# Two edits to a two-layer hybrid backbone kernel: query and gate units of the last layer's projection without context columns, and the recurrent stage's level products on VectorE

## The reference

```python
IN_SIZES = (HG_W, HG_W, HG_W, HG_W, HG_W, GQA_W, GQA_KV_W, GQA_KV_W, NA_W, NA_W, NA_W)
# = 256 x5 (q, f_fwd, f_bwd, i, g) | 384, 128, 128 (q, k, v) | 384 x3 (q, k, v)
for l in range(DEPTH):
    need_ctx = l < DEPTH - 1
    ...
    y_lat, y_ctx = mixing_sublayer(...)      # y_ctx is None if not need_ctx
```

## Time and profile before

| | |
|---|---|
| median of 3 runs | 4626.42 us (4623.34 to 4635.23) |
| the profiled execution, its own time | 4631.18 us |
| its span, first to last instruction | 4629.5 us |
| mean granted TensorE clock | 0.905 of full |
| PE busy, DVE, ACT, POOL | 83%, 44%, 23%, 11% of the span |
| `project_in(1)` | from 2560 to 2903 us in the span, 343 us |
| `hgrn` of layer 0 | from 457 to 639 us, 182 us |
| `hgrn` of layer 1 | from 2909 to 3058 us, 149 us |

### The profile page before, as it was taken

One profiled execution on the slowest core, in us unless ns is written; L12 is line 12 of the kernel. 1 busy time (PEld: TensorE's weight loads), 2 busy tenths in 40 slices (PEclk: granted clock), 3 DMA queues, 4 the chain that ended last, 5 costly groups with the idle time before them and its releaser, 6 DMA issues. The chain is left out here.

```text
span 4629.5 us, 55289 instructions
## 1 busy us (share of the span) xinstructions
PE 3859.6 (83%) x22802; PEld 3059.9 (66%) x22802; DVE 2037.8 (44%) x2175; ACT 1087.3 (23%) x1434; POOL 492.6 (11%) x314
## 2 busy tenths in 40 slices
PE   3998468939785999999996899469767859999996
PEld 2887336438674888888884788345356647777774
DVE  3111657645423343444345121667656234544445
ACT  1000332425314111111114000332345131111113
POOL 1000403002005000000003000511022040000000
PEclk6999679968897999999997999679889879999998
DMA  5222430041223101111105222240132211111111
GB/s 185 82 82 79 156 134 21 12 108 23 86 77 123 42 27 41 41 35 32 41 18 164 80 82 78 104 141 5 46 82 68 66 63 51 41 54 41 51 35 73
DMA packets 339917, 320.39 MB, mean 69 GB/s; under 512 B 42718, under 2 KB 310602, under 8 KB 339786
## 3 DMA queue, kind: packets, MB, share of 16 engines
q1 hardware_dynamic: 297514, 265.07, 18.5%
q0 software_dynamic: 6912, 31.46, 2.3%
q10 hardware_dynamic: 35360, 22.02, 1.5%
HBM read 248.17 MB, written 73.30 MB: 69 GB/s over the span
## 5 line engine op out<-in xcount | busy, mean ns | idle before, releaser
L477 PE MATMUL psum<-h_hi,f_whi 128*128 128x512 f32 (+1 forms) x1760 | 485.1, 373 | 70.7 <-DVE f_wlo L922 70.7
L927 DVE TENSOR_TENSOR y<-y,psum 128x1280 f32<-128x1280 f32 (+1 forms) x352 | 476.8, 1355 | 109.3 <-PE psum L477 103.9
L477 PE MATMUL psum<-h_lo,f_whi 128*128 128x512 f32 (+1 forms) x1760 | 481.6, 371 | 0.0
L477 PE MATMUL psum<-h_hi,f_wlo 128*128 128x512 f32 (+1 forms) x1760 | 481.4, 371 | 0.0
L477 PE MATMUL psum<-h_hi,w_hi 128*128 128x512 f32 x1472 | 379.2, 364 | 118.2 <-DVE w_lo L543 118.2
L477 PEld LDWEIGHTS psum<-h_hi,f_whi 128*128 128x128 f32 x1760 | 306.8, 188 | 135.0 <-DVE f_wlo L922 71.2
L477 PE MATMUL psum<-h_lo,w_hi 128*128 128x512 f32 x1472 | 377.4, 363 | 0.0
L477 PE MATMUL psum<-h_hi,w_lo 128*128 128x512 f32 x1472 | 377.0, 362 | 0.0
L922 DVE TENSOR_TENSOR f_wlo<-f_raw,f_whi 128x1024 fp32r<-128x1024 f32 x132 | 161.0, 1221 | 481.9 <-ACT f_whi L893 423.5
L477 PEld LDWEIGHTS psum<-h_hi,w_hi 128*128 128x128 f32 x1472 | 249.9, 190 | 164.3 <-issue 119.1
L893 ACT CAST f_whi<-f_raw 128x1024 fp32r<-128x1024 f32 x132 | 138.4, 1048 | 907.3 <-PE psum L477 882.5
(11 more groups left out here) (264 smaller groups left out, 5706.9 us busy)
## 6 DMA issues: line engine op xcount, KB each, us to landing
f_raw<-in_w_ffn_in SPq DMA_DIRECT2D x88, 512.0 KB, 6.0
proj_cm<-lin_stage POOLq DMA_DIRECT2D x48, 640.0 KB, 4.1
w_raw<-in_w_in SPq DMA_DIRECT2D x48, 512.0 KB, 5.0
ada_w<-in_w_ada SPq DMA_DIRECT2D x24, 1024.0 KB, 10.8
f_raw<-in_w_ffn_out SPq DMA_DIRECT2D x44, 512.0 KB, 3.6
ln_x<-x_cm SPq DMA_DIRECT2D x18, 1024.0 KB, 7.9
att_raw<-proj_cm SPq DMA_DIRECT2D x48, 320.0 KB, 5.7
x_cm<-ln_x SPq DMA_DIRECT2D x14, 1024.0 KB, 4.4
```

The costliest lines, as they stand in the source:

```text
L477: ins = nc.tensor.matmul(out[:, t0:t0 + tn], w, h[:, t0:t0 + tn], start=start and n == 0, stop=stop and n == 2)
L927: nc.vector.tensor_tensor(y[:, o, 0:tokens], y[:, o, 0:tokens], sets(o), ALU.add).then_inc(s_acc.h, 1)
```

## The change

1. `linear` gets an optional list of widths. With it, the units are written out one after another in every engine's stream instead of a loop over pairs, and a unit's matmuls, PSUM copy and store cover only its width. `project_in` gives such a list for the last layer alone: 1024 tokens for the ten units named above, 1280 for the other fourteen.
2. In `hgrn`, both layers, DVE makes all four products of a level and the decays. GpSimd keeps only the making of the mask.
3. The block loads start with the two query blocks, ACT takes their `silu` before the sigmoids, and DVE makes the first query arrays between the key arrays.
4. The modulation pieces are spread over five levels, not six, and their turn goes from between the levels and the key transposes into the chain of state additions, behind step 13.
5. At the end ACT takes all logarithms first and then all exponentials, and DVE's `result` of all groups comes after the gates.

```diff
+CTX_QUERY_UNITS = (0, 1, 8, 9, 10, 11, 12, 15, 16, 17)
+def each_unit(e, n, body):
+    for u in range(n):
+        body(u, u % 2, u // 2)
-def linear(k, src, units, tokens, h_hi, h_lo, y, split=False):
+def linear(k, src, units, tokens, h_hi, h_lo, y, split=False, widths=None):
+    in_turn = each_unit if widths else in_pairs
+    def width(u):
+        return widths[u] if widths else tokens
...
-                    nc.vector.tensor_copy(dst, sets[s][:, 0:tokens]).then_inc(s_ev.h, 1)
+                    nc.vector.tensor_copy(dst, sets[s][:, 0:width(u)]).then_inc(s_ev.h, 1)
...
-                        ins = three_products(nc, sets[s], chunks, w_hi[:, s, cols], w_lo[:, s, cols],
+                        ins = three_products(nc, sets[s], token_chunks(width(u)), w_hi[:, s, cols], w_lo[:, s, cols],
                                              h_hi[:, j], h_lo[:, j], j == 0, j == KB - 1)
...
-                for i in (2, 3, 4, 5, 0, 1, 6, 7, 8, 9):
+                for i in (0, 1, 2, 3, 4, 5, 6, 7, 8, 9):
                     sp.dma_start(pj[:, i], k.pj_dram[:, HG_COL // P + i]).then_inc(s_ld[i].h, 16)
...
-                    for u in range(n_m * lvl // LEVELS, n_m * (lvl + 1) // LEVELS):
+                    for u in range(n_m * lvl // (LEVELS - 1), n_m * (lvl + 1) // (LEVELS - 1)) if lvl < LEVELS - 1 else ():
                         mod.copy(act, u)
...
-                def root(gi):
+                def log(gi):
                     after(act, s_ms, gi + 1)
-                    g = groups[gi]
-                    nc.scalar.activation(group(rs, g), k.psum[:, gi % 2].rearrange("p (b t) -> p b t", b=2), ACT.Ln, bias=k.eps[:]).then_inc(s_ln.h, 1)
-                    after(act, s_ln, gi + 1)
-                    nc.scalar.activation(group(rs, g), group(rs, g), ACT.Exp, scale=-0.5).then_inc(s_rs.h, 1)
+                    nc.scalar.activation(group(rs, groups[gi]), k.psum[:, gi % 2].rearrange("p (b t) -> p b t", b=2), ACT.Ln, bias=k.eps[:]).then_inc(s_ln.h, 1)
...
+                for gi in range(len(groups)):
+                    after(act, s_ln, gi + 1)
+                    nc.scalar.activation(group(rs, groups[gi]), group(rs, groups[gi]), ACT.Exp, scale=-0.5).then_inc(s_rs.h, 1)
...
+                for lvl in range(LEVELS):
...
+                        nc.vector.tensor_tensor(same(k_new, lvl), same(k_old, lvl), of_same(lvl, True), ALU.mult).then_inc(s_uk.h, 1)
+                        nc.vector.tensor_tensor(same(q_new, lvl), same(q_old, lvl), of_same(lvl, False), ALU.mult).then_inc(s_uq.h, 1)
+                    after(dve, s_ck, lvl + 1)
+                    scored(dve, 1)
...
+                        nc.vector.tensor_tensor(diff(ok, lvl), diff(k_old, lvl), of_diff(lvl, True), ALU.mult).then_inc(s_ok.h, 1)
                     after(dve, s_cq, lvl + 1)
...
+                        nc.vector.tensor_tensor(diff(oq, lvl), diff(q_old, lvl), of_diff(lvl, False), ALU.mult).then_inc(s_oq.h, 1)
+                        decays(lvl + 2)
                     if lvl:
                         out(lvl - 1)
...
-                mod.turn(pe)
                 for s in (s_uk, s_ck, s_ok):
                     after(pe, s, LEVELS)
...
                     if i % 4 == 1 and i // 4 < n_sets:
                         products(i // 4)
+                    if i == 13:
+                        mod.turn(pe)
...
 def project_in(k, l, h_hi, h_lo):
+    context = [NT] * (IN_W // P)
+    for u in CTX_QUERY_UNITS:
+        context[u] = SEQ
+    linear(k, lambda u: w_in[:, :, bass.ds(u * P, P)], IN_W // P, NT, h_hi, h_lo, None, widths=context if l == DEPTH - 1 else None)
```

More of the change, by code:

```diff
@@ L504, in store @@
                         pool.wait_ge(s_ev.h, s_ev.at(3) + u)
[L505 to L507 removed]
+                        pool.dma_start(k.pj_dram[:, bass.ds(u, 1), 0:width(u)].rearrange("p a t -> p (a t)"),
+                                       stage[:, s, 0:width(u)]).then_inc(s_st[s].h, 16)
+                    in_turn(pool, units, store)
                     for s in range(2):
@@ L518, in load @@
                     sp.dma_start(raw[:, s].rearrange("p (j q) -> p j q", j=KB), src(u)).then_inc(s_w[s].h, 16)
-                in_pairs(sp, units, load)
+                in_turn(sp, units, load)
             @block.scalar
@@ L558, in _ @@
                     lo(s + 2, s)
-                with dve.Fori(1, (units - 2) // 2) as i:
-                    for s in range(2):
-                        evac(i * 2 + s, s)
-                        lo(i * 2 + s + 2, s)
-                for u in range((units - 2) // 2 * 2, units):
+                if not widths:
+                    with dve.Fori(1, (units - 2) // 2) as i:
+                        for s in range(2):
+                            evac(i * 2 + s, s)
+                            lo(i * 2 + s + 2, s)
+                for u in range(2 if widths else (units - 2) // 2 * 2, units):
                     evac(u, u % 2)
@@ L2128, in _ @@
                     nc.scalar.activation(pj[:, 2 + i], pj[:, 2 + i], ACT.Sigmoid).then_inc(s_sig.h, 1)
-                for blk in range(2):
-                    after(act, s_ld[blk], 16)
-                    nc.scalar.activation(pj[:, blk], pj[:, blk], ACT.Silu).then_inc(s_q.h, 1)
                 for i in range(TT // 2):
@@ L2227, in out @@
                                                   k.psum[:, 2 * slot:2 * slot + 2, 0:ne * CHUNK].rearrange("p h (e t) -> p h e t", t=CHUNK)).then_inc(s_ev.h, 1)
-                for lvl in range(LEVELS - 1):
-                    old, new = uq[:, lvl % 2], uq[:, (lvl + 1) % 2]
+                for lvl in range(LEVELS):
+                    last = lvl == LEVELS - 1
+                    k_old, k_new, q_old, q_new = uk[:, lvl % 2], uk[:, (lvl + 1) % 2], uq[:, lvl % 2], uq[:, (lvl + 1) % 2]
+                    for s in (s_ck, s_uk, s_ok, s_cq, s_uq, s_oq):
+                        after(dve, s, lvl)
+                    after(dve, s_k, 4)
@@ L2230, in _ @@
                     decay_ready(dve, lvl)
-                    after(dve, s_cq, lvl)
-                    after(dve, s_uq, lvl)
-                    after(dve, s_oq, lvl)
-                    after(dve, s_k, 4)
                     if lvl:
                         scored(dve, lvl + 1)
-                    nc.vector.tensor_tensor(same(new, lvl), same(old, lvl), of_same(lvl, False), ALU.mult).then_inc(s_uq.h, 1)
-                    after(dve, s_cq, lvl + 1)
-                    nc.vector.tensor_tensor(diff(oq, lvl), diff(old, lvl), of_diff(lvl, False), ALU.mult).then_inc(s_oq.h, 1)
+                    if last:
+                        nc.vector.tensor_tensor(half(k_new, 0), half(k_old, 0), of_half(1), ALU.mult).then_inc(s_uk.h, 1)
+                        nc.vector.tensor_tensor(half(q_new, 1), half(q_old, 1), of_half(0), ALU.mult).then_inc(s_uq.h, 1)
+                    else:
+                        nc.vector.tensor_tensor(same(k_new, lvl), same(k_old, lvl), of_same(lvl, True), ALU.mult).then_inc(s_uk.h, 1)
+                        nc.vector.tensor_tensor(same(q_new, lvl), same(q_old, lvl), of_same(lvl, False), ALU.mult).then_inc(s_uq.h, 1)
@@ L2240, in _ @@
                     if lvl:
                         out(lvl - 1)
-                last = LEVELS - 1
-                old, new = uq[:, last % 2], uq[:, (last + 1) % 2]
-                decay_ready(dve, last)
-                after(dve, s_cq, last)
-                after(dve, s_uq, last)
-                after(dve, s_oq, last)
-                scored(dve, last + 1)
-                nc.vector.tensor_tensor(half(new, 1), half(old, 1), of_half(0), ALU.mult).then_inc(s_uq.h, 1)
-                after(dve, s_cq, last + 1)
@@ L2251, in _ @@
-                nc.vector.tensor_tensor(half(oq, 0), half(old, 0), of_half(DL + 1), ALU.mult).then_inc(s_oq.h, 1)
-                out(last - 1)
-                out(last)
+                out(LEVELS - 1)
                 for t in range(1, TT, 2):
@@ L2302, in _ @@
                         gated(gi - 1)
-                    if gi >= 2:
-                        result(gi - 2)
                 gated(len(groups) - 1)
-                result(len(groups) - 2)
-                result(len(groups) - 1)
+                for gi in range(len(groups)):
+                    result(gi)
             @block.tensor
@@ L2439, in hgrn @@
     s_mk.done(16)
-    for s in (s_msk, s_t1):
-        s.done(1)
+    s_msk.done(1)
     for s in (s_sig, s_f, s_k, s_qi):
@@ L2445, in hgrn @@
         s.done(2)
-    s_t.done(LEVELS - 1)
+    s_t.done(LEVELS)
     for s in (s_uk, s_ck, s_ok, s_uq, s_cq, s_oq):
```

88 lines of the change are left out of this document (33 added, 55 removed).

## The result

| | before | after |
|---|---|---|
| median of the runs compared | 4625.96 us (4 runs) | 4577.51 us (4 runs, 4571.11 to 4582.9) |
| ratio, 95% interval | 1 | 0.9887 (0.9872 to 0.9902) |
| the profiled execution, its span | 4631.18, 4629.5 us | 4582.9, 4580.9 us |

What follows compares the result with a forecast made beforehand. Projection bound by TensorE alone, recurrent stages by each level's circle of latencies; 32.0 + 15.1 + 15.6 = 62.7 us off the profiled 4631.18, so the median 4626.42 becomes 4564 us (forecast alone 4550 to 4578), range 4549 to 4590.

Steps and rivals of the forecast that it cites:

- The projection: Last layer's input projection, bound by TensorE: ten narrow units at 10.88 instead of 14.08 us save 32.0 us, code fetch nothing.
- The recurrent stage: Both `hgrn` stages, bound by a latency circle per level: gains of 15.1 us in layer 0 and 15.6 in layer 1.
- start to level 2's scores: Start of `hgrn`: products at 1.49 us without GpSimd beside them bring these scores 4.0 us earlier in layer 0, 7.2 in layer 1.
- levels 2 to 6: Four level circles shorter, with keys' products covered by ACT's copies: gain 2.7 us in layer 0, 1.8 in layer 1.
- last scores to the transposes: Stretch before the key transposes, where only the last `out` remains in layer 0: gain 8.9 us, in layer 1 2.5.
- the turn in the additions: Moved turn behind step 13 of the state additions, partly covered: exposed 6.0 us in layer 0, 0.9 in layer 1.
- the end: End of `hgrn`, two table loads instead of ten for five groups: gain 5.5 us in layer 0, 5.0 in layer 1.
- 4 us a layer: Far end for the lowest levels' products: cost if they take 2.55 us, seen only beside GpSimd, instead of 1.49.
- Moving the query blocks ahead in the load queue costs nothing: Start of `hgrn`: ACT's ten passes and one exposed load are the same in another order; cost zero.
- VectorE as the bound of the levels: Rival: keys' products don't fit beside ACT's copies, circles up to 3 us longer, 4594 us in all; chance 0.08.

Runs made afterwards that it cites:

- p1: Kernel before with only the last layer's input projection written out, ten units over 1024 tokens: 4600.98 us against 4629.66, ratio 0.9933.
- p2: Changed kernel with its projection as before (loop, all units 1280 tokens), so only the recurrent edits: 4610.23 us, ratio 0.9954 to the kernel before.
- p4: Kernel before with only the end of the recurrent stage changed: all logarithms, then all exponentials, results last; ratio 0.9978.
- p8: Kernel before with all level products and decays on VectorE; load order, pieces, turn and end as they were; ratio 0.9976.
- p3: Kernel before with the last layer's projection written out unit by unit, every unit still 1280 tokens; ratio 1.0008.
- p7: Changed kernel with other operand patterns in the first level's four products, numbers not the reference's; one execution, 4581.5 us.
- p5: Changed kernel with the turn of the modulation rows put back between the levels and the key transposes; ratio 0.9898 to the kernel before.
- p6: Changed kernel with the turn moved behind the last pieces, ahead of the last level's scores: 4569.22 us, ratio 0.9883 to the kernel before.
- p11: Changed kernel with level copies ahead of modulation copies, pieces behind four levels, turn behind level 5's scores: 4552.34 us against 4631.22 before, ratio 0.983.

## Why the prediction was right, and where it was off

The 14.1 us between 62.7 and 48.6 are 11.6 too much from the recurrent stages and 4.3 lost in the stage behind the first of them, less 1.5 more from the projection and 0.3 from the rest. The range was wide enough for it.

**The projection** was right in mechanism and size: 32.0 predicted, 33.5 in after, 31.7 in p1, with both unit prices met to 0.01 us. With the old loop the stage took 353.89 to 355.70 us (before, p2, p4, p8), with the narrow units 322.13 to 323.94 (all the others but p3), so 1.5 us above the sum is within what it does by itself. Nothing was paid for the written-out code (p3).

**The recurrent stage** was right in sign and too high in size: 30.7 predicted, 19.1 found. Step by step (gains in us; stretches between the starts of the named matmuls):

| step | layer 0: predicted, found | layer 1: predicted, found |
|---|---|---|
| start to level 2's scores | 4.0, 0.8 | 7.2, 2.4 |
| levels 2 to 6 | 2.7, 1.5 | 1.8, 2.2 |
| last scores to the transposes | 8.9, 8.5 | 2.5, 2.5 |
| the turn in the additions | -6.0, -5.9 | -0.9, -4.3 |
| the end | 5.5, 7.0 | 5.0, 5.3 |

(The transposes themselves, for which the sum had nothing, took 0.7 us more in layer 1.)

- *The start failed*: the sum took 1.49 us for the products of the first level, because the trace of before had 2.55 only beside GpSimd, and company was taken for a cause. Without GpSimd they are 2.55 to 2.58, and p7 shows the decays' pattern to be the cause. The prediction kept this as the far end, "4 us a layer": in layer 1 four products of 1.07 us too much make 4.3 of the 4.8 that are missing. In layer 0, p7's second key product waited 2.06 us for scores of TensorE, so there the fault is smaller: by p7's times with both `diff` products at 1.49 the queries' one would end 36.5 us into the stage, in after it ends at 39.2, an estimate of 2.7 of the 3.2 missing.
- *A second zero of the start fell too.* "Moving the query blocks ahead in the load queue costs nothing" left out VectorE, which makes the query arrays ahead of the last key arrays. By p8 the new order costs 1.1 to 2.1 us at level 2's scores of layer 0, and 0.7 to 1.3 in layer 1. In layer 0 it overlaps with the fault of the first level, because VectorE waits there for TensorE's scores, so the two don't simply add. In layer 1 they exceed the 4.8 missing by 0.2 to 0.8 us, which is within what the stage does by itself.
- *The turn in layer 1 failed in its size*: the price of 1.95 us was read at the clock's upper level. In its new place it ran at 0.50 and took 3.57. Even with no cover at all that is 3.6 of the 4.3; the rest lies in the additions behind it, at the same clock. Work moved to another place takes that place's clock. In layer 0 the granted clock over the turn hardly changed with the move, 0.73 before and 0.71 in after, so the old 7.35 us were nearly the new price (7.56), and -6.0 was right.
- *The turn's move was worth nothing even where it was forecast well.* The 8.9 and the -6.0 of layer 0 stood in the sum as two terms. p5 shows that 6.9 us of turn are exposed in either place; what was won between the last scores and the transposes besides comes from the pieces that no longer stand there. No term put both places side by side.
- *The levels* fell short by 1.2 us in layer 0. From level 2's scores to the last it is 58.8 us in after, but 59.8 in p2, 56.8 in p7 and 55.5 in p5, whose levels are the same from there on. Two thirds of what p5 is shorter lie in the circle shown above: TensorE's pause of 0.71 us, and its clock over the pieces (0.79 in after, 1.00 in p5). A term of 2.7 can't be told from that in one execution.
- *The end* gave 1.5 us more in layer 0. The exponentials end 22.7 us after the first state part, 29.6 before, 6.9 us; forecast were 6.3, less 0.8 for stores that come together. From the last exponential to the next stage are 3.9 us in after and 4.0 before, so the stores cost nothing. By the Trainium skill (ScalarE: Activation LUTs, Table sets: the hidden batching unit) one load would serve logarithm and exponential; after has two, at 606.96 and 618.06, and the second stands in the last group's chain, as the sum had it by the rows of before.
- *The next stage was left out.* `gqa_prepare` of layer 0 lost 4.3 us. Its last four rotation matmuls (L1812, 128x512) took 3.78 us where the same ones took 1.98 in p6. In after and then in p6:

```profile
655.66 3.78 PE L1812 MATMUL psum<-gq_pj,rot_gain 128*128 128x512 f32 x4
```

```profile
648.21 1.98 PE L1812 MATMUL psum<-gq_pj,rot_gain 128*128 128x512 f32 x4
```

Over the first row the granted clock is 0.50, over the second 1.00, its two levels. The four explain 1.8 us; in after TensorE is at 0.50 for all of 647 to 665 us, in p6 it is back at 1.00 when these four run, and the rest lies in the other work of that stretch. The stage took 44.6 to 46.0 us in after, p2, p5 and p7, and 40.5 to 43.1 in before and in all other experiments. What in the stage ahead decides it was not singled out.

Of the rivals, VectorE as the bound of the levels didn't come at its price, since the circles got shorter in both layers. In layer 0 VectorE waits for ScalarE in the circle. In layer 1 it is nearly full: in circles of 9.6 to 9.8 us it stands 0.9 to 1.0 us for TensorE and at most 0.4 for ScalarE. The recurrent part was won by two of its four edits (p4, p8). By the stages the others together lost 6.5 us of it again, if the parts add up, which the whole-kernel times don't show and p4 and p8 in one kernel would have to. Of the others only the turn was tried alone (p5).

## What to carry to other kernels

When a filler (here the modulation pieces) is put into a latency circle, look at every engine that it passes, not only at the one that has room: TensorE had the time, but ScalarE served the filler ahead of the circle, and swapping two groups of copies gave 9 us in one stage. Work that is moved must be costed in the new place beside the old one, at the new place's clock; in layer 0 the best place for the turn was the one gap in which all other engines were at work and no filler stood. And a duration that is seen only under contention proves nothing about its cause: cost it at both ends, and ask first what else in the instruction differs.

## What was not expected of the hardware

- A VectorE product of 128x1280 fp32 takes 1.49 us also where the first operand and the output are blocks of single elements, but 2.56 us when each next element of the second operand comes from the other half of an array, 2561 elements off (p7).
- The same 48 small matmuls of the turn took 6.3 us (p11), 7.6 (after), 8.7 (p5) and 9.1 (p6), by their place. The granted clock over them was 0.86, 0.71, 0.61 and 0.58: the time goes with the clock.
- In dense streams of 64x64 matmuls TensorE pauses with "issue" as the only cause, for up to 3.3 us in the levels (p11) and up to 4.4 in the first scores (p6). In the levels the places differ from program to program; in layer 0's first scores the long pause ends 27.2 to 27.7 us into the stage in the five programs with the old order, and 28.9 to 29.4 in the eight with the new one. The written-out projection, with 128x512 matmuls, shows no such pause over 12 packets of instructions. Waits for code would fit this, but no run shows that they are.
